# 104 more products on the tensor engine behind the last weight product of a two-block transformer kernel

## The reference, cut to what matters

```
x = first_block(x, ...)          # two layers: projections, attention, gated output
return second_block(x, ...)      # feed forward, mixer, feed forward, and last:
    gate = jax.nn.sigmoid(rmsnorm_2(h, ple_pre_g[i]) @ w_ple_gate[i])
    h = h + rmsnorm_2(gate * (p[i] @ w_ple_proj[i]), ple_post_g[i])
```

## Time and profile before

| what | value |
|---|---|
| median of the timings | 2877.51 us |
| the profiled execution, its own time | 2878.4 us |
| its span, first to last instruction | 2876.5 us |
| granted TensorE clock, mean | 0.999 of full speed |
| PE busy, share of the span | 2856.0 us, 99% |
| PEld busy | 2387.2 us, 83% |
| DVE busy | 1726.8 us, 60% |
| ACT busy | 1296.8 us, 45% |

### The profile page before, as it was taken

One profiled execution on the slowest core, in us unless ns is written; L12 is line 12 of the kernel. 1 busy time (PEld: TensorE's weight loads), 2 busy tenths in 40 slices (PEclk: granted clock), 3 DMA queues, 4 the chain that ended last, 5 costly groups with the idle time before them and its releaser, 6 DMA issues.

```text
span 2876.5 us, 33211 instructions
## 1 busy us (share of the span) xinstructions
PE 2856.0 (99%) x13488; PEld 2387.2 (83%) x13488; DVE 1726.8 (60%) x1649; ACT 1296.8 (45%) x1340; POOL 14.4 (1%) x20
## 2 busy tenths in 40 slices
PE   9999999999999999999999999999999999999998
PEld 8878888888898888888888888888888888888887
DVE  5469856455566655555555677676755555555575
ACT  5344545454444533333333455645533333333354
POOL 0000000000000000000000000000000000000000
PEclk9999999999999999999999999999999999999999
DMA  7545355555455655555555557443655555555554
GB/s 250 191 156 190 117 186 182 192 177 173 157 158 199 205 190 190 190 190 190 190 190 190 189 178 253 161 150 125 221 191 191 191 191 185 192 190 191 193 179 154
DMA packets 275999, 530.60 MB, mean 184 GB/s; under 512 B 8768, under 2 KB 32464, under 8 KB 275392
## 3 DMA queue, kind: packets, MB, share of 16 engines
q1 hardware_dynamic: 274864, 527.01, 54.7%
q0 software_dynamic: 752, 2.04, 0.2%
q10 hardware_dynamic: 288, 0.20, 0.0%
HBM read 527.12 MB, written 2.10 MB: 184 GB/s over the span
## 4 chain that ended last, share of the span: by engine, by line
PE 95%; DVE 2%; ACT 1%; DMA 1%; issue 0%; SPq 0%; DVEq 0%; ACTq 0%
PE ps L695 29%; PE ps L696 29%; PE ps L698 27%; PE ps L704 2%; PE ps L891 1%; PE ps L723 1%; PE ps L791 1%; DVE w_lo L2046 1%; PE ps L724 1%; PE ps L728 1%; ACT w_hi L1404 1%; PE ps L879 1%; PE ps L919 1%; DMA raw<-in_w_in 0%; PE ps L825 0%
## 5 line engine op out<-in xcount | busy, mean ns | idle before, releaser
L2046 DVE TENSOR_TENSOR w_lo<-raw,w_hi 128x2048 fp32r<-128x2048 f32 (+3 forms) x505 | 1125.1, 2231 | 716.1 <-ACT w_hi L1404 714.3
L1404 ACT ACTIVATE w_hi<-raw 128x2048 fp32r<-128x2048 f32 (+3 forms) x505 | 941.7, 1868 | 975.8 <-DMA raw<-in_ff_w_down 320.5
L695 PE MATMUL ps<-w_hi,x_hi 128*128 128x512 f32 (+4 forms) x3168 | 1229.1, 388 | 5.5 <-DVE w_lo L2046 4.4
L696 PE MATMUL ps<-w_lo,x_hi 128*128 128x512 f32 (+4 forms) x3168 | 1217.3, 384 | 0.0
L698 PE MATMUL ps<-w_hi,x_lo 128*128 128x512 f32 (+3 forms) x2944 | 1130.8, 384 | 0.0
L695 PEld LDWEIGHTS ps<-w_hi,x_hi 128*128 128x128 f32 x3168 | 595.0, 188 | 123.6 <-DVE w_lo L2046 5.4
L696 PEld LDWEIGHTS ps<-w_lo,x_hi 128*128 128x128 f32 x3168 | 595.3, 188 | 112.8
L698 PEld LDWEIGHTS ps<-w_hi,x_lo 128*128 128x128 f32 x2944 | 552.7, 188 | 108.6
L695 PE MATMUL ps<-w_hi,h_hi 128*128 128x512 f32 x640 | 249.1, 389 | 0.0
L698 PE MATMUL ps<-w_hi,h_lo 128*128 128x512 f32 x640 | 249.0, 389 | 0.0
L696 PE MATMUL ps<-w_lo,h_hi 128*128 128x512 f32 x640 | 249.0, 389 | 0.0
(11 more groups left out here) (340 smaller groups left out, 1559.6 us busy)
## 6 DMA issues: line engine op xcount, KB each, us to landing
raw<-in_w_in SPq DMA_DIRECT2D x139, 1024.0 KB, 4.9
raw<-in_ff_w_gate SPq DMA_DIRECT2D x88, 1024.0 KB, 5.0
raw<-in_ff_w_up SPq DMA_DIRECT2D x88, 1024.0 KB, 5.0
raw<-in_ff_w_down SPq DMA_DIRECT2D x88, 1024.0 KB, 5.1
raw<-in_w_out SPq DMA_DIRECT2D x45, 1024.0 KB, 5.1
raw<-in_w_ple_gate SPq DMA_DIRECT2D x16, 1024.0 KB, 5.0
raw<-in_w_in SPq DMA_DIRECT2D x8, 696.0 KB, 4.1
raw<-in_w_in SPq DMA_DIRECT2D x8, 520.0 KB, 3.7
```

What stands on the lines that cost most here:

```text
L695: nc.tensor.matmul(o, x[0][:, k0 + c, s], hi[:, c, 0:width], start=first and c == 0, stop=False)
L696: nc.tensor.matmul(o, x[0][:, k0 + c, s], lo[:, c, 0:width], start=False, stop=False)
L1404: nc.scalar.activation(landed_part(w_hi, u, j), landed_part(raw, u, j), ACT.Copy).then_inc(hi_ready, 1)
L2046: V.tensor_tensor(landed_part(w_lo, u, j), landed_part(raw, u, j), landed_part(w_hi, u, j).bitcast(F32), ALU.subtract).then_inc(parts_read ...
```

## The change

Behind the last call of `product_of_tile`, TensorE gets thirteen more calls of a new local function, each of which issues eight products. They read `x_hi` and slot 0 of `w_hi`, write banks 4 and 5 (the second form bank 4 alone), wait for no semaphore and raise none. Nobody reads what they write. The forms differ in the shape or the layout of an operand. Nothing else in the kernel is changed.

```
+            def unused(held, moving, columns, start=True, bank=None):
+                for n in range(8):
+                    o = ps[0:held.shape[-1], 4 + n % 2 if bank is None else bank, 0:columns]
+                    nc.tensor.matmul(o, held, moving, start=start, stop=True, skip_group_check=True)
+
+            held = x_hi[:, 0, 0:P]
+            row = w_hi[:, 0, :]
+            unused(held, row[:, 0:BW], BW)
+            unused(held, row[:, 0:BW], BW, start=False, bank=4)
+            unused(held, row[:, 0:2 * BW:2], BW)
+            unused(held, row[:, 8:8 + BW], BW)
+            unused(held, row[:, 0:1].to_broadcast([P, BW]), BW)
+            unused(held, row[:, 0:496], 496)
+            unused(held, row[:, 0:448], 448)
+            unused(row[:, 0:P], x_hi[:, 1, :], SEQ)
+            unused(row[:, 0:64], x_hi[:, 1, :], SEQ)
+            unused(x_hi[0:64, 0, 0:P], row[0:64, 0:BW], BW)
+            unused(x_hi[:, 0, 0:64], row[:, 0:BW], BW)
+            unused(held, row[:, 0:BW].rearrange("p (a b) -> p b a", a=32), BW)
+            unused(held, x_hi[:, 2:4, :], BW)
```

## The result

The changed kernel takes 2895.85 us (2895.34 to 2896.36, two timings) against 2877.51 us before: ratio 1.0058, 95% interval 1.0042 to 1.0074. It is slower by 18.3 us, and within 2% of the kernel before. The forecast was 2891.5 us with a range of 2889.2 to 2896.8; so the time lies inside, 4.3 us above the forecast, between the sizes of rival A.

What follows compares the result with a forecast made beforehand. TensorE was taken to bound the kernel, with some 8 us free behind its last needed product. The 21.70 us of new products would add 14.0 us to 2877.5 us, giving 2891.5 us, range 2889.2 to 2896.8.

Steps and rivals of the forecast that it cites:

- rival A: On TensorE, the array waits for a moving operand with gaps; three sizes, 2893.1, 2894.7 or 2896.6 us; chance 0.38 together.
- the cover: Behind the last needed product, some 8 us in which TensorE's work is free while DVE, ACT and SyncE finish.
- The sum: All 104 new products on TensorE, priced by the step between starts, with the row changes: 21.70 us.
- Forms 3 and 12: New products with moving columns 8 and 64 bytes apart: 3.63 us at the plain step, upper end 6.88 us.
- the change to 64 rows: Switching the new products to 64 rows and back: 0.1 us a change, 0.2 us for two.
- form 11: Eight new products with 512 moving and 64 stationary columns: step 0.222 us, 1.78 us in all.
- forms 6 and 7: New products with slightly fewer than 512 moving columns: steps 0.220 and 0.200 us, 1.76 and 1.60 us.
- Forms 1 and 2: New products with 512 moving columns, the second adding to one bank: the kernel's own step of 0.2266 us.
- the meeting of the engines: At the end of the program, behind TensorE's drain: 0.3 us.
- Rivals B: The end does not wait for TensorE (2877.5 us, chance 0.01), or equal loads are dropped (2890.0 us, chance 0.07 with shorter steps).
- C: New products do not overlap, 0.58 us each, 60 us: 2930 us; chance 0.02 together with other costs above 2897 us.
- D: Time lost fetching the new instructions on TensorE: one stop at most, some 0.4 us; no separate chance given.

Runs made afterwards that it cites:

- e1_plain32: The changed kernel with 32 plain products (512 contiguous moving columns) in place of the thirteen calls: 2877.67 us, ratio 1.0001 to the kernel before.
- e2_plain104: The changed kernel with 104 plain products in place of the thirteen calls: 2893.02 us, ratio 1.0053 to the kernel before.
- e9_plain_for_gaps: The changed kernel with plain products replacing the two calls whose moving columns have gaps, still 104 products: 2892.13 us, ratio 1.0050 to the kernel before.
- e4_moving: The changed kernel with nineteen groups of 16 products, differing in the moving operand's layout, in place of the thirteen calls: steps of 0.216 to 0.462 us.
- e5_lines: The changed kernel with seventeen groups varying how many elements come from one 16 bytes: fp32r steps 0.216 to 0.452 us, float32 0.429 to 0.900 a record.

## Why the prediction was right, and where it was off

- What bounds the kernel, and where the cover ends: right. The program ends with the later of SyncE and TensorE's drain; below 8.0 us of work nothing is seen (e1_plain32), above it each microsecond counts in full (e2_plain104). The cover came out at 8.0 us, as the earlier trace rows gave it.
- The sum: 21.70 us forecast. In the trace after, the first new product starts at 2868.65, the last at 2893.89, 25.2 us, where 21.70 - 0.23 = 21.5 were forecast: 3.8 us more. The term that was mis-sized is "Forms 3 and 12", 3.63 us at the lower end. They took 8 x 0.450 = 3.60 and 8 x 0.432 = 3.46 us, together 7.06, 3.4 us more, and 0.2 beyond the upper end of 6.88 that I had. e9_plain_for_gaps puts plain products in their place and gives back 3.42 us in the trace. I took the row that was nearest by type, contiguous fp32r; what mattered was the layout, of which no row before speaks.
- The other 0.4 us of the sum are the change to 64 rows (some 0.4 instead of 0.2 for the pair), form 11 at 0.230 instead of 0.222, the shift of form 4 at 0.234, and 0.05 us in forms 6 and 7 together; form 5 (0.218) gives back 0.07. Forms 1 and 2 had the step of 0.2266 exactly, and form 13 from its second step on (the first, behind form 12, took 0.257).
- Beyond the sum, the last needed product started 0.43 us later than before (2868.42 against 2867.99) and the meeting of the engines took 0.2 us less than I had set. 3.8 + 0.4 - 0.2 = 4.0 us on the span, 2894.5 against 2890.5. The rest up to 4.3 us is that the median lies 0.5 us below the profiled execution, and not 0.9 as before.
- Rival A was the right mechanism, and in its second size: form 3 pays as well. It was put at 2894.7 us; on top come the 0.2 us beyond the upper end, the 0.4 us of the small forms and the later start. The upper end of the range, 2896.8, came from its largest size (form 12 at 0.86), which did not occur; that the time lies only 1 us inside owes something to luck. The rival's reason was wrong in one point: I held form 3 for the milder case, and it costs more than form 12.
- Rivals B, C and D: the drain held the end, no load was dropped (13592 loads, 104 more), the products overlapped, and the 104 products of e2_plain104 in one block show no stop for instructions.

What stood behind the mis-sized term is the layout of the moving operand; that is shown. How the layout makes the step is worked out from the series and not shown directly: the steps go as if the moving operand were read in aligned pieces of 16 bytes, about 1.77 ns for each. The plain product has 128 of them, 128 x 1.77 = 0.2266 us. Form 3 has 256: 0.452. Form 12 has 512, but pieces with a single element cost about half in fp32r (0.432 to 0.461 for 512), and in float32 they don't (0.857 to 0.900). That the kernel's own step is itself set by reading, not by the array, is suggested by e4_moving, where half the pieces (each element twice) gave 0.216 and a single one (one column read 512 times) 0.218. But two places read in turn, which come to 512 pieces by the same count, gave 0.216 too, so the count is not the whole of it.

The Trainium skill, page "Advanced Engine Details and Errata", section "SBUF Cachelines", names the same unit of 16 bytes, and e4_moving and e5_lines sort by it. By its rule of at least two hits form 3 would have been free; here two hits in a line cost 0.452 us and four 0.227, so the measurement decides.

The Trainium skill, page "TensorE: Matmul & The Clock Gate", section "Back-to-back issue gap", gives 215.8 ns for an isolated gap at 512 columns. Here 0.216 us is the step when each element is read twice or two places are read in turn; a plain operand takes 0.2266, in 104 products in a row.

## What to carry to other kernels

Price a product by the step between starts, and look at the moving operand's layout first. For orders that go forward in fp32r and float32, the types that ran here, count the aligned 16-byte pieces that its columns come from, at some 1.77 ns each; a gap that leaves two of four columns unread halves the rate in fp32r (0.227 to 0.452 us for 512 columns). Plain float32 has a lower bound of 0.429 us a record, which hides such a gap (0.450). Gaps in the stationary operand are all but free with 512 moving columns, so where one of the two operands must be read with gaps, let it be the stationary one. Work put behind the last needed product is free only up to the length of the tail, and the drain at the end of an engine's list tells when it ended.

## What the hardware showed that I had not expected

- Every second column (8 bytes apart) is not milder than every fourth, or than the order with neighbours sixteen apart: 0.452, 0.461 and 0.432 us.
- A moving operand that begins 1, 2 or 8 columns further costs 3 to 4% (0.236, 0.233, 0.234 us), one that begins 16 columns further 1% (0.228).
- Two places read in turn are faster than one contiguous operand, 0.216 against 0.227 us; eight in turn are slower than any other fp32r order that ran, 0.491. Why stays open.
- Stationary operands of 32, 64 or 96 columns take 0.230 us, slightly more than 128 columns do.
